# First layer of a two-layer trunk: both query units in one pass, low halves last, activations before weights

## The reference, cut to what matters

```
h = x
for i in range(2):
    xn = rms_norm(h, norm_mix[i])
    h = h + hybrid_mixer(xn, w_in[i], ...)      # q, k, v, u, conv inputs, gates are columns of xn @ w_in
    xn = rms_norm(h, norm_ffn[i])
    h = h + (swiglu(xn, ...) if i == 0 else moe_swiglu(xn, ...))
return rms_norm(h, final_norm)
```

## Time and profile before

| what | value |
|---|---|
| median of 3 runs | 1556.78 us (1555.36 to 1557.28) |
| the profiled execution's own time | 1555.8 us |
| its span | 1554.0 us |
| PE busy | 1516.3 us, 98% |
| DVE busy | 597.5 us, 38% |
| ACT busy | 347.9 us, 22% |
| POOL busy | 218.2 us, 14% |

### The profile page before, as it was taken

One profiled execution on the slowest core, in us unless ns is written; L12 is line 12 of the kernel. 1 busy time (PEld: TensorE's weight loads), 2 busy tenths in 40 slices (PEclk: granted clock), 3 DMA queues, 4 the chain that ended last, 5 costly groups with the idle time before them and its releaser, 6 DMA issues.

```text
span 1554.0 us, 30325 instructions
## 1 busy us (share of the span) xinstructions
PE 1516.3 (98%) x13463; PEld 924.6 (59%) x13463; DVE 597.5 (38%) x925; ACT 347.9 (22%) x427; POOL 218.2 (14%) x283
## 2 busy tenths in 40 slices
PE   7999999999999999999999999999999999999996
PEld 6987999999999988994333333333333323333331
DVE  5887577655556477554120201211202012011021
ACT  5452345434445552341000000000000000000001
POOL 3446369300000147100000000000000000000000
PEclk9999999999999999999999999999999999999999
DMA  9732394655554522478999999999999999999995
GB/s 274 232 107 82 92 283 163 209 180 174 190 191 156 176 76 82 134 273 340 386 396 419 419 419 419 419 419 420 418 420 419 419 419 420 419 419 404 419 419 244
DMA packets 146339, 465.00 MB, mean 299 GB/s; under 512 B 10144, under 2 KB 92064, under 8 KB 131872
## 3 DMA queue, kind: packets, MB, share of 16 engines
q1 hardware_dynamic: 143296, 461.40, 76.9%
q0 software_dynamic: 416, 1.05, 0.3%
q10 hardware_dynamic: 2496, 0.61, 0.3%
HBM read 461.98 MB, written 1.05 MB: 298 GB/s over the span
## 4 chain that ended last, share of the span: by engine, by line
PE 58%; DMA 7%; SPq 3%; DVE 1%; ACT 1%; issue 0%; DVEq 0%; ACTq 0%
PE work L1118 14%; PE acc L1136 13%; PE work L729 12%; PE acc L1118 11%; DMA ring<-in_moe_w_down 4%; DMA ring<-in_moe_w_gate 3%; PE ssm_y L1118 3%; SPq L629 3%; PE acc L1073 1%; PE acc L1086 1%; PE work L850 1%; PE ssm_y L857 1%; PE acc L729 0%; PE acc L820 0%; PE work L994 0%
## 5 line engine op out<-in xcount | busy, mean ns | idle before, releaser
L729 PE MATMUL work<-xs,parts 128*128 128x256 f32 x3600 | 454.7, 286 | 8.9 <-DVE xs L1485 5.0
L729 PEld LDWEIGHTS work<-xs,parts 128*128 128x128 f32 x3600 | 441.6, 193 | 19.7 <-issue 16.4
L1118 PE MATMUL work<-ring,arena 128*32 128x448 f32 x2688 | 276.1, 539 | 0.3 <-DMA ring<-in_moe_w_up 0.3
L1136 PE MATMUL acc<-ring,arena 128*32 128x512 f32 x2352 | 258.9, 593 | 11.2 <-DMA ring<-in_moe_w_down 9.5
L1478 DVE TENSOR_TENSOR parts<-ring,parts 128x2048 fp32r<-128x2048 f32 x94 | 220.0, 2345 | 123.7 <-ACT parts L1212 123.5
L1118 PE MATMUL acc<-ring,arena 128*32 128x448 f32 x2048 | 216.5, 540 | 1.6 <-ACT arena L1398 0.7
L1212 ACT ACTIVATE parts<-ring 128x2048 fp32r<-128x2048 f32 x94 | 178.8, 1908 | 90.0 <-PE work L729 62.5
L1136 PEld LDWEIGHTS acc<-ring,arena 128*32 128x32 f32 x2352 | 74.5, 110 | 191.3 <-issue 164.3
L1118 PEld LDWEIGHTS work<-ring,arena 128*32 128x32 f32 x2688 | 87.3, 110 | 165.8 <-issue 160.6
L1885 DVE TENSOR_TENSOR arena<-arena,work 128x448 f32<-128x448 f32 x42 | 23.7, 615 | 350.9 <-ACT arena L1398 350.9
L1398 ACT ACTIVATE arena<-acc 128x448 f32<-128x448 f32 x32 | 15.7, 541 | 637.0 <-PE work L1118 637.0
(11 more groups left out here) (312 smaller groups left out, 1069.6 us busy)
## 6 DMA issues: line engine op xcount, KB each, us to landing
ring<-in_moe_w_gate SPq DMA_DIRECT2D x128, 896.0 KB, 21.6
ring<-in_moe_w_up SPq DMA_DIRECT2D x128, 896.0 KB, 22.9
ring<-in_moe_w_down SPq DMA_DIRECT2D x112, 1024.0 KB, 22.7
ring<-in_w_in SPq DMA_DIRECT2D x44, 1024.0 KB, 6.2
ring<-in_dense_w_gate SPq DMA_DIRECT2D x14, 1024.0 KB, 5.4
ring<-in_dense_w_up SPq DMA_DIRECT2D x14, 1024.0 KB, 5.1
ring<-in_dense_w_down SPq DMA_DIRECT2D x14, 1024.0 KB, 4.9
ring<-in_w_out SPq DMA_DIRECT2D x8, 1024.0 KB, 12.7
```

The lines of the kernel that those rows point to most:

```text
L729: last = nc.tensor.matmul(out_ap, a, b, start=start and n == 0, stop=stop and n == len(pairs) - 1, skip_group_check=shared)
L1118: last = nc.tensor.matmul(banks[g][GRP * q:GRP * q + GRP, 0:CHUNK], x, w[:, q * CHUNK:q * CHUNK + CHUNK], start=k == 0, stop=k == KT - 1, ...
L1136: last = nc.tensor.matmul(acc[GRP * q:GRP * q + GRP, b, :], eh[:, which, 2 * u + kk, g * GRP:g * GRP + GRP], w[:, kk, half * OUT_COLS:half ...
```

## The change

There are five edits, all in the first layer. PE makes q0 and q1 together: for each feature tile k it makes the high x high and high x low products of both units, which need only the high halves of the weights, and after the eighth tile all low x high products, first q0's and then q1's (`first_queries`). The number of products stays 96. DVE makes the tokens before any weight's low half; ACT splits q1's high half before the tokens' high half. SP loads q1 before it waits for the parameters. PE gets 12 idle products between the first sum of squares and q0. The doubling of the table from 64 to 128 columns moves from behind v1 to behind u0.

```diff
@@ block.sync
-                if n == 1:
+                if n == 2:
                     sp.wait_ge(params_loaded, 16 * PARAMS)
@@ sum_squares
-                if l:
-                    idle_products(9)
+                idle_products(9 if l else 12)
+
+            def first_queries(bank):
+                banks = [bank, begin(Group((0, "q", 1)))]
+                high, low = [[unit_view(parts[:, n, h, :], f"q{n}") for n in range(2)] for h in range(2)]
+
+                def part(n, q):
+                    return banks[n][:, q * L:q * L + L]
+
+                for k in range(KT):
+                    await_x(0, k)
+                    for n in range(2):
+                        pe.wait_ge(hi_ready, n + 1)
+                        for q in range(2):
+                            w = high[n][:, k, q * P:q * P + P]
+                            accumulate(part(n, q), [(w, x_parts[h][:, k, :]) for h in range(2)],
+                                       start=k == 0 and q == 0, stop=False, shared=True)
+                for n in range(2):
+                    pe.wait_ge(lo_ready, n + 1)
+                    for k in range(KT):
+                        for q in range(2):
+                            last = accumulate(part(n, q), [(low[n][:, k, q * P:q * P + P], x_parts[0][:, k, :])],
+                                              start=False, stop=k == KT - 1, shared=True)
+                    last.then_inc(work_done, 1)
@@ block.scalar
             splits.upto_first(1)
             root_mean_square(0, 0)
+            splits.upto_first(2)
             x_high(xnT, xn_ready, lambda k: k + 1)
             splits.upto_first(AHEAD)
@@ block.vector
-            splits.upto_first(1)
             normalise(0, 0)
             splits.upto_first(AHEAD)
...
-            TABLE_AT = [(("v", 0), 4), (("v", 0), 8), (("v", 1), 16), (("v", 1), 32), (("v", 1), 64)]
+            TABLE_AT = [(("v", 0), 4), (("v", 0), 8), (("v", 1), 16), (("v", 1), 32), (("u", 0), 64)]
```

More of the change, by code:

```diff
@@ L776, in _ @@
                 for kind, t in STEPS:
-                    if kind in ("gelu", "softplus") or (l, kind, t) == (0, "wo", KT - 1):
+                    if kind in ("gelu", "softplus") or (l, kind, t) in ((0, "wo", KT - 1), (0, "q", 1)):
                         continue
@@ L785, in _ @@
                         bank = None if g is None else begin(g)
-                    if kind in ("q", "k", "u", "h", "b", "c"):
+                    if (l, kind, t) == (0, "q", 0):
+                        first_queries(bank)
+                    elif kind in ("q", "k", "u", "h", "b", "c"):
                         w = weights(l, f"{kind}{t}")
```

## The result

The changed kernel took 1560.35 us (median of 16 runs, 1557.59 to 1561.9). Beside it on the same chips the kernel before took 1556.67 us (16 runs, 1554.68 to 1559.68). The ratio is 1.0022 with a 95% interval of 1.0015 to 1.0029, so the change made the kernel 0.22% slower. The profiled execution took 1558.45 us, its span 1556.7; that is 2.65 us more than the profiled execution before.

The account below looks back on a forecast made before the run. PE, busy 98% of the span, was taken as the bound. Front -2.8, wait before k1 +3.6, k1's clock +1.95, the rest -0.6 made 1555.8 + 2.2 = 1558.0; the median, 1.0 higher, gave 1559.0 us, range 1555.5 to 1561.5.

Parts of the forecast that it names:

- the landing of q1: SP's early load of q1 lands near 13.6 us, nothing charged; rival of a late landing: 1561.0 us, chance 0.14.
- One for one to the end: After 88 us no PE wait exceeds 1.1 us until the experts, so PE's earlier gain or loss reaches the end.
- The front: PE makes q0 and q1 from 17.16 to 28.9 us at full clock and is 2.8 us ahead at k0.
- the prediction's own signs of being wrong: Wait before k1 under 2 us, PEclk at 1.00 in k1, or q1's high half on ACT starting after 14.3 us.
- The bound from rows: On SP's loads, at 290 GB/s q1 takes 3.6 us; the parameters land by 15.0 us even behind it; nothing charged.
- In front of k1: PE's wait before k1 grows from 0.76 to 4.3 us, then a clock loss of 1.95 us in k1.
- the chain: DVE's parameter chain, behind three low halves, begins 0.83 us later at 28.6; ACT's sines, q0's copy and k1 follow.
- the sum: Up to the convolution: front -2.8, wait before k1 +3.6, clock in k1 +1.95, b0, c0 and convolution -0.6: 2.2 us later.
- Behind v0: The wait of 2.67 us before b0 goes, one of 2.3 before c0 comes; PE 1.9 to 2.6 us late.
- the dearer of the two values named: c0 ends at 87.9 us with a clock loss of 1.49 us, at 86.4 without.
- Both kinds of hold: Behind c0, DVE's convolution puts PE at least 1.9 us behind even if c0 keeps the clock; c0's clock loss makes 2.6.
- The sentence that moving the table buys little: Table of 64 behind u0: DVE has the same work up to c0's low half in either order, so little is gained.

Follow-up runs that it names:

- the angles first on the kernel before: The kernel before with the parameters' exponential on ACT and DVE's angle chain moved ahead of the tokens, nothing of the change: 1556.45 us, ratio 0.9995.
- the front alone: The changed kernel with the table of 64 put back behind v1: 1557.52 us, ratio 1.0012.
- warm start: Six idle products around the first transposes, ahead of the sum of squares: on the changed kernel 1559.55 us; on another variant with tables moved earlier 1550.01 us.
- the table alone: The kernel before with the table of 64 moved behind u0 and nothing else: 1557.39 us, ratio 1.0005.

## Why the prediction was right, point by point

The forecast named the right mechanism and a time within 1.4 us. One of its steps failed, the landing of q1, and part of the agreement is luck; both are told below.

**One for one to the end.** From the tail's start to the end of the execution it was 1555.8 - 85.26 = 1470.5 us before and 1558.45 - 87.86 = 1470.6 after; in nine of the other traces it was 1470.1 to 1471.1. It was 1471.4 with the angles first on the kernel before, 1471.6 with idle products before c0, and 1473.4 with idle products before k1, where the half clock stood behind the tail. In the traces before and after, all of the change's effect is made in the first 88 us.

**The front.** The tokens did not come sooner, and PE made 144 products in 17.5 us with the clock at 1.00. The step that failed is q1's landing, which the prediction costed at nothing: it said 13.6 us by the rate of the earlier trace rows, ahead of 14.25, and ACT waited for it until 14.95, so q0 started at 17.88 us instead of 17.16 (0.57 us of that is the landing). This trips one of the prediction's own signs of being wrong, a high half of q1 that starts later than 14.3 us. The reading behind it took the small number of bytes after 10 us for idle DMA engines; the same row has their busy share at 0.70. In the other traces with the new order, the early load and the short sum of squares, ACT's wait for q1 was between nothing and 0.38 us, so the 0.57 is at the long end. The parameters were late too, though nothing waited for them: SP waited 10.5 us instead of 9.6.

```profile
SPq L613 <- DMA convw<-in_conv_w: 10.5, 1, 10.5
```

In the ten traces with q1 loaded early this wait was 10.2 to 11.1 us, in the four others 9.1 to 9.6, so q1's load does delay the parameters. The page of the Trainium skill named in the prediction, "DMA: Bandwidth & Descriptors" ("Queues, rings and completion order"), has the engines alternate between queues; these waits agree with it. That the parameters delay q1 in turn is not shown, since no run loads q1 alone. The bound from rows was too low by 1.3 us for q1.

**In front of k1.** This step held: a wait of 4.26 us where 4.3 was named. Over eight traces with different fronts k1 started 21.75 to 21.77 us behind q0 while PE's own work there took 17.5 to 19.8 us; and without the chain the wait was gone. The half clock came, and cost 7.47 - 5.98 = 1.49 us where the sum had 1.95. (The prediction took 5.87 us for a unit at full clock, half of a row of 96; a row of 48 takes 5.98.) At v0 PE was 2.83 us behind (46.95 against 44.12), and the prediction said 2.8. That near-equality is luck. It is made of q0's start +0.72 where nothing was charged, the way from q0 to k1 +0.63 (21.77 less 21.14) where 0.83 was, and the clock +1.49 where 1.95 was: three errors of size that cancel.

**Behind v0.** b0 without a wait, c0 with 2.45 us (2.3 named) and 7.46 us of products, DVE's wait for b0's high half 1.39 us (1.0 named), and the tail at 87.86, the dearer of the two values named (86.4 or 87.9). PE is 2.59 us late at the convolution (1.9 to 2.6), which DVE had ready at 93.52, 0.7 us before. Both kinds of hold are shown: with c0's half clock removed PE waits 1.20 us there and gains nothing. The sentence that moving the table buys little holds for the waits and not for the clock. Against the front alone the move lost 1.5 us in the trace. PE's wait is as long in both, 2.47 us before b0 there and 2.45 before c0 here; what differs is the clock behind it (c0's 48 products took 7.46 us, against 5.98 at full clock). On DVE the move adds the wait for b0's high half, so that c0's low half starts 60.25 us behind q0 instead of 58.97. The wait before c0 was followed by the half clock in seven of the eight traces with the table there and no idle products in that wait; with the table at v1 a wait of over 2 us before b0 was followed by it in one of three. Why it follows in one case and not in another is open.

**The size.** The trace gave +2.65 us where the sum had +2.2: at v0 +2.83 as above, from there to the tail -0.23, where the sum had -0.6 up to the convolution, and 0.05 behind it. The medians gave +3.7. The missing 1.0 us is of a kind that one trace can't show: both profiled executions had the short sum of squares (3.69 us). In 6 of the 12 traces without a warm start it took 5.75 to 6.16 us. From its start to q0 the kernel before needs 7.6 us with the short one, and with the long one the table alone, which has the same front, needs 8.3. With the front of the change it is 7.5 to 8.2 us with the short one (four traces, mean 7.9) and 9.7 to 9.95 with the long one (four traces, mean 9.85); left out is the run that loads q1 late. Before, q0's low half stood in front of the tokens on DVE and covered a late norm; in the change a high half of 1.9 us always follows the norm. So the long sum costs about 2.0 us with the change and 0.7 without. With the long sum in half of the executions that makes 0.6 us on average. But the profiled execution of the change was itself the slowest of the short ones, 8.15 us, so only about 0.4 us of the missing 1.0 is accounted for. That is worked out from few traces, not shown by a run, and the rest stays open.

## What to carry to other kernels

Before crediting a faster front on one engine, find what starts the first wait behind it: if that chain lies on other engines, the gain turns into a longer wait, and the half clock can follow that wait. An edit that moves work past a chain of small operations should first ask whether the chain itself can go where its engine is idle; here that was worth 5.7 us, and closing three more idle stretches of DVE, with the table of 64 back behind v1, another 4.8 us between the medians of two different chips. Where executions differ in how late an input comes, look at what covered that lateness before taking the cover away.

## What the runs showed of the hardware

- The same 16 passes of the sum of squares, started at 9.3 to 9.95 us, took 3.69 us in some executions and 5.75 to 6.16 in others (mean of a matmul 384 and 538 to 569 ns), while PEclk read 1.00 in both. The ratio, 1.56 to 1.67, is like that of the half clock elsewhere (6 or 7 products of 256 columns in a microsecond at 0.50, 10 or 11 at 1.00), so I take it for a half clock that the rows don't show; this is argued, not shown. The Trainium skill, "TensorE: Matmul & The Clock Gate" ("Part 1: The HAM clock gate"), has the engine start throttled and released by activity, which fits the durations and not the PEclk rows.
- A wait of 2.2 to 2.5 us was followed by the half clock in some traces and not in others (c0 at 7.46 us behind 2.45, and at 5.98 behind 2.45). Once it followed a wait of 1.96 us (k1 at 7.48, without idle products in the front), and once one of 1.20 us (the gates, with idle products before k1). Where the half clock came behind a wait of 1.96 to 2.5 us, the 48 products took 7.35 to 7.49 us instead of 5.98.
- Filling a wait with idle products so that less than 1.8 us of it was left kept the clock each time, at no cost to the product behind it: k1 started 21.76 us behind q0 with 16 of them and without. Where 4.88 us were left behind the 12 idle products (q1 behind the parameters), the clock fell to 0.50 all the same and the front took 19.48 us.
- Loading 1 MB on SP's queue while the small parameter loads were under way held those up by 0.6 to 2.0 us: SP's wait for them was 10.2 to 11.1 us in ten traces with that load and 9.1 to 9.6 in four without.
